# A transformer block with 32 routed experts on one core: token-wise gather, split scatter, reordered expert products and 4 MB weight loads

## The reference

```
h2 = rms_norm(x1, norm2_g, NORM_EPS).reshape(B * S, D)
logits = (x2 @ w_router + b_router)
top_vals, top_idx = lax.top_k(logits, TOP_K)          # 4 of 32 experts
top_w = jax.nn.softmax(top_vals, axis=-1)
combine = einsum('tk,tke->te', top_w, one_hot(top_idx, 32))
for e in range(32):
    h = x2 @ w_up[e] + b_up[e]                        # (256, 2048)
    glu, lin = h[..., :1024], h[..., 1024:]
    glu = minimum(glu, 7.0); lin = clip(lin, -7.0, 7.0)
    a = glu * sigmoid(1.702 * glu) * (lin + 1.0)
    out = out + combine[:, e:e+1] * (a @ w_down[e] + b_down[e])
return x1 + out
```

## Time and profile before

| what | value |
|---|---|
| time, median of 3 runs | 1219.95 us (1217.81 to 1220.06) |
| time of the profiled execution | 1219.87 us |
| span of the profiled execution | 1218.1 us |
| mean granted TensorE clock | 0.978 of full |
| PE busy | 1169.7 us (96%) |
| DVE busy, ACT busy | 339.1 us (28%), 266.9 us (22%) |
| HBM read | 448.12 MB, 369 GB/s over the span |
| front part, up to the first up product of item 1 | 288.8 us |
| item 1 to 32, up to the last down product | 288.8 to 1211.0 us |

### The profile page before, as it was taken

The page is one execution under the profiler, slowest core; times in us unless marked ns, Lnnn a source line. Parts: engine busy times, 40 slices in busy tenths (PEclk is TensorE's granted clock), DMA queues, the critical chain, the costliest instruction groups (busy, mean ns, idle before and its releaser), DMA issues.

```text
span 1218.1 us, 15891 instructions
## 1 busy us (share of the span) xinstructions
PE 1169.7 (96%) x6786; PEld 562.5 (46%) x6788; DVE 339.1 (28%) x625; ACT 266.9 (22%) x407; POOL 84.7 (7%) x101
## 2 busy tenths in 40 slices
PE   8999999997999999999999999999999999999998
PEld 7789988884333333333333333333333333333332
DVE  5767865655111111111111111111121111111112
ACT  6765454442111111111111111111111111111110
POOL 6333340001000000000000000000000000000000
PEclk9999999998999999999999999999999999999999
DMA  8454469858999999999999999999999999999991
GB/s 313 151 169 149 151 246 361 304 217 330 382 425 429 428 428 428 427 428 426 429 427 427 428 428 429 426 427 428 427 428 428 427 427 428 428 426 427 428 405 66
DMA packets 51476, 450.16 MB, mean 370 GB/s; under 512 B 4610, under 2 KB 4738, under 8 KB 26836
## 3 DMA queue, kind: packets, MB, share of 16 engines
q1 hardware_dynamic: 49936, 447.76, 89.1%
q10 hardware_dynamic: 1476, 1.42, 0.4%
HBM read 448.12 MB, written 1.05 MB: 369 GB/s over the span
## 4 chain that ended last, share of the span: by engine, by line
PE 85%; DVE 10%; ACT 2%; issue 1%; POOL 1%; DMA 0%; DVEq 0%; SPq 0%; POOLq 0%; ACTq 0%
PE aux L1604 37%; PE aux L1661 20%; PE acc L1448 11%; PE aux L1537 4%; PE acc L1441 3%; PE acc L1587 3%; PE aux L1635 2%; DVE lin L1228 2%; DVE sig L1232 2%; DVE glu L1224 2%; DVE lin L1225 2%; PE aux L1615 1%; DVE w_lo L880 1%; PE aux L1650 1%; PE aux L1644 1%
## 5 line engine op out<-in xcount | busy, mean ns | idle before, releaser
L1604 PE MATMUL aux<-ring,xgT 128*64 128x512 f32 x2048 | 458.2, 594 | 0.8 <-DVE xgT L1164 0.8
L1604 PEld LDWEIGHTS aux<-ring,xgT 128*64 128x64 f32 x2048 | 140.5, 137 | 266.4 <-issue 258.0
L1661 PE MATMUL aux<-ring,aT 128*64 128x512 f32 x1024 | 245.3, 635 | 0.0
L1224 DVE TENSOR_SCALAR glu<-aux 128x512 f32<-128x512 f32 x32 | 22.1, 692 | 483.3 <-PE aux L1604 483.3
L1661 PEld LDWEIGHTS aux<-ring,aT 128*64 128x64 f32 x1024 | 77.0, 147 | 148.7 <-issue 147.1
L845 ACT ACTIVATE sig<-glu 128x512 f32<-128x512 f32 x32 | 20.1, 630 | 474.9 <-DVE glu L1224 474.9
L880 DVE TENSOR_TENSOR w_lo<-raw,w_hi 128x1024 fp32r<-128x1024 f32 x80 | 104.3, 1324 | 50.0 <-ACT w_hi L662 50.0
L662 ACT ACTIVATE w_hi<-raw 128x1024 fp32r<-128x1024 f32 x80 | 84.1, 1059 | 88.6 <-PE acc L1448 73.0
L1587 PE MATMUL acc<-y_sb,pick_wT 64*128 64x512 f32 x256 | 98.2, 628 | 0.8 <-ACT y_sb L853 0.8
L1448 PE MATMUL acc<-w_hi,hT_hi 128*128 128x512 f32 x188 | 75.7, 403 | 1.4 <-DVE hT_lo L892 1.3
L1448 PE MATMUL acc<-w_hi,hT_lo 128*128 128x512 f32 x188 | 73.3, 390 | 0.0
(11 more groups left out here) (292 smaller groups left out, 920.1 us busy)
## 6 DMA issues: line engine op xcount, KB each, us to landing
ring<-w_up_dram SPq DMA_DIRECT2D x128, 2048.0 KB, 22.9
ring<-w_down_dram SPq DMA_DIRECT2D x64, 2048.0 KB, 21.9
raw<-w_in_dram SPq DMA_DIRECT2D x25, 1024.0 KB, 5.2
raw<-w_branch_dram SPq DMA_DIRECT2D x6, 1024.0 KB, 5.2
raw<-w_kv_dram SPq DMA_DIRECT2D x4, 1024.0 KB, 5.2
raw<-w_out_dram SPq DMA_DIRECT2D x4, 1024.0 KB, 5.3
x<-x_dram SPq DMA_DIRECT2D x2, 512.0 KB, 4.3
raw<-w_in_dram SPq DMA_DIRECT2D x2, 512.0 KB, 6.4
```

The source lines that it names most:

```text
L1224: nc.vector.tensor_scalar(glu[:], bank_glu[:], LIMIT, None, ALU.min).then_inc(glu_ready, 1)
L1604: ins = nc.tensor.matmul(bank[64 * half:64 * half + 64, :], xgT[:, k], w_rows[:, c0 + half * W:c0 + (half + 1) * W], start=(k == 0), stop= ...
L1661: ins = nc.tensor.matmul(bank_cy[64 * half:64 * half + 64, :], aT[:, j, 64 * ff_half:64 * ff_half + 64], w_rows[:, half * W:(half + 1) * W ...
```

## The change

- **Gather by tokens.** `x1` itself (float32) is the moving operand and `pick` (float32, scaled with the token's rstd) the stationary one: 4 products of 512 columns give the 64 gathered rows in `bank_cy`. ACT copies them to `xg_tok` (the room of `sig`), PE turns them with 4 transposes (`turn_gathered`), and DVE multiplies them into `xgT`. `m_parts` and the work that made it (ACT, POOL, DVE) go. The gather stands behind `k == 3`, the transposes behind `k == 5`.
- **Scatter.** The item's output is scaled by its weight per slot (`slot_w`) and split by ACT (`y_hi`) and DVE (`y_lo`) into two float32r parts; the scatter is 8 float32r products with a 0/1 matrix `pickT`, all behind the next item's up products. The two transposes of `pick_w` move into the middle of the down products.
- **Glu columns first.** For `k` 6 and 7 all products of `bank_glu` are issued before those of `bank_lin`, with a semaphore of their own (`glu_done`); DVE multiplies `glu` with the sigmoid before it clamps `lin`.
- **Match-replace.** The top-4 set is found with one `match_replace` per tile of tokens in place of index search, comparison and reduction.
- **Ring.** 12 units of 16 KB per partition; an expert is 2 chunks of `w_up` (4 MB, 32 KB per partition) and 2 of `w_down` (2 MB), 8 chunks (two experts) are held. The two first `w_up` chunks are loaded in halves.

```diff
-UP_ROWS, DOWN_ROWS = 2, 4
+UP_ROWS, DOWN_ROWS = 4, 4
 UP_CHUNKS, DOWN_CHUNKS = KD // UP_ROWS, KD // DOWN_ROWS
 CHUNKS = UP_CHUNKS + DOWN_CHUNKS
-RING = 11
-WARM_UP, KEEP_UP = 14, 8
-NEG = -1.0e30
+UNITS, CHUNK_UNITS = 12, (2, 2, 1, 1)
+RING = 2 * CHUNKS
+FIRST_UNIT = [UNITS // 2 * (s // CHUNKS) + sum(CHUNK_UNITS[:s % CHUNKS]) for s in range(RING)]
+HALVED = 2
...
                     src = w_down[bass.ds(expert, 1), c * n:(c + 1) * n, :].rearrange("o (p j) n -> p (o j n)", p=P)
-                sp.dma_start(ring[:, slot], src).then_inc(slot_loaded[slot], 16)
+                sp.dma_start(chunk_tile(slot), src).then_inc(slot_loaded[slot], 16)
 
             def load_next(g):
                 load_chunk(g % RING, g % CHUNKS, g // CHUNKS)
@@ -460,22 +468,20 @@
                     sp.wait_ge(aux_ready, JOB["mem_y", MEM_H - 1] + 1)
                     block_read(sp, ("cb",))
                 if p in (27, 29, 31, 33):
-                    load_next((p - 27) // 2)
+                    n = (p - 27) // 2
+                    load_half_chunk(n // 2, n % 2)
                 if p == 35:
                     sp.wait_ge(half_used, 2 * LAST_PIECE[("proj", 1, 1)] + 2)
...
+            sp.wait_ge(half_used, 2 * NP)
             load_next(5)
-            for g, last in ((6, NP - 3), (7, NP - 1)):
-                sp.wait_ge(lo_done, 2 * last + 2)
-                load_next(g)
-            sp.wait_ge(half_used, 2 * NP)
-            load_next(8)
-            load_next(9)
+            load_next(6)
             sp.wait_ge(logits_ready, 1)
-            sp.wait_ge(parts_pool, 2)
-            sp.wait_ge(parts_dve, 2)
-            load_next(10)
+            load_next(7)
             for g in range(RING, NEXP * CHUNKS):
                 chunk_used(sp, g - RING)
...
-                nc.scalar.activation(top_e[:, t], top_v[:, t, 0:TOPK], ACT.Exp, bias=ntop[:, t:t + 1],
-                                     accum_out=top_den[:, t, 0:1]).then_inc(soft_ready, 1)
-
-
-            nc.scalar.activation(aT[:, 0], ident[:], ACT.Copy).then_inc(aT_ready, 1)
-            nc.scalar.activation(y_sb[:, 0:P], ident[:], ACT.Copy).then_inc(y_ready, 1)
...
+
+            copy_gathered(1)
 
             def item(n):
+                copy_gathered(n + 1)
+                act.wait_ge(xg_turned, n + 1)
                 act.wait_ge(glu_ready, n)
                 nc.scalar.activation(sig[:], glu[:], ACT.Sigmoid, scale=ALPHA).then_inc(sig_ready, 1)
                 act.wait_ge(aT_done, n)
                 nc.scalar.activation(aT[:].rearrange("p k s -> p (k s)"), bank_t[:], ACT.Copy).then_inc(aT_ready, 1)
-                act.wait_ge(pick_wT_done, n)
-                act.wait_ge(scattered, 4 * n)
-                nc.scalar.activation(pick_wT[:].rearrange("p t s -> p (t s)"), bank_t[:, 0:NT * P],
-                                     ACT.Copy).then_inc(pick_wT_ready, 1)
+                act.wait_ge(pickT_ready, n)
                 act.wait_ge(y_done, n)
-                nc.scalar.activation(y_sb[:], bank_cy[:], ACT.Copy).then_inc(y_ready, 1)
+                nc.scalar.activation(y_hi[:], bank_cy[:], ACT.Copy, scale=slot_w[:, 0:1]).then_inc(y_hi_ready, 1)
 
...
-                ins = nc.vector.max_index(top_i[:, t], top_v[:, t], logits[:, t])
+                ins = nc.vector.match_replace(out=others[:, t], in_to_replace=top_v[:, t], in_values=logits[:, t],
+                                              imm_value=-HUGE)
             chained(ins)
-            chained(nc.vector.tensor_copy(top_f[:], top_i[:]))
+            nc.vector.tensor_scalar(chosen3[:, :, 0], others[:], -HUGE, None, ALU.is_equal).then_inc(chosen_ready, 1)
...
+            def move_gathered(n):
+                dve.wait_ge(xg_turned, n)
+                order = "p (h q) -> p q h"
...
+                dve.wait_ge(glu_done, n)
+                nc.vector.tensor_scalar(glu[:], bank_glu[:], LIMIT, None, ALU.min).then_inc(glu_ready, 1)
+                dve.wait_ge(glu_ready, n)
+                dve.wait_ge(sig_ready, n)
+                nc.vector.tensor_tensor(sig[:], glu[:], sig[:], ALU.mult).then_inc(gated_ready, 1)
                 dve.wait_ge(up_done, n)
-                nc.vector.tensor_scalar(glu[:], bank_glu[:], LIMIT, None, ALU.min).then_inc(glu_ready, 1)
-                nc.vector.tensor_scalar(lin[:], bank_lin[:], LIMIT, -LIMIT, ALU.min, ALU.max).then_inc(up_read, 1)
-                dve.wait_ge(glu_ready, n)
-                dve.wait_ge(up_read, n + 1)
-                nc.vector.scalar_tensor_tensor(lin[:], lin[:], 1.0, glu[:], ALU.add, ALU.mult
-                                               ).then_inc(glin_ready, 1)
-                dve.wait_ge(glin_ready, n)
-                dve.wait_ge(sig_ready, n)
-                nc.vector.tensor_tensor(sig[:], lin[:], sig[:], ALU.mult).then_inc(a_ready, 1)
-
-                dve.wait_ge(gathered, n + 1)
-                move_gathered()
+                nc.vector.tensor_scalar(bank_lin[:], bank_lin[:], LIMIT, -LIMIT, ALU.min, ALU.max
+                                        ).then_inc(lin_ready, 1)
+                dve.wait_ge(gated_ready, n)
+                dve.wait_ge(lin_ready, n)
+                nc.vector.scalar_tensor_tensor(sig[:], bank_lin[:], 1.0, sig[:], ALU.add, ALU.mult
+                                               ).then_inc(a_ready, 1)
+
+                move_gathered(n + 1)
+                build_pick_w(bass.ds(n - 1, 1))
                 build_pick(bass.ds(n + 1, 1))
+
                 dve.wait_ge(pick_wT_done, n)
-                build_pick_w(bass.ds(n, 1))
+                nc.vector.tensor_scalar(pickT[:].rearrange("p t s -> p (t s)"), bank_t[:, 0:NT * P], 0.0, None,
+                                        ALU.is_gt)
+                nc.vector.tensor_reduce(slot_w[:], bank_t[:, 0:NT * P], AX, ALU.add).then_inc(pickT_ready, 1)
                 dve.wait_ge(y_done, n)
                 build_bias_sel(bass.ds(n, 1))
+                dve.wait_ge(pickT_ready, n)
+                dve.wait_ge(y_hi_ready, n)
+                nc.vector.scalar_tensor_tensor(y_lo[:], bank_cy[:], slot_w[:, 0:1], plain_f32(y_hi[:]),
+                                               ALU.mult, ALU.subtract).then_inc(y_lo_ready, 1)
...
+            def gather(n):
+
+                pe.wait_ge(pick_ready, n)
...
-                                                   stop=(t == NT - 1 and m == 2), skip_group_check=True)
+                    for half in range(2):
+                        ins = nc.tensor.matmul(bank_cy[64 * half:64 * half + 64, :], pick[:, t],
+                                               x1[:, t, half * W:(half + 1) * W],
+                                               start=(t == 0), stop=(t == NT - 1), skip_group_check=True)
                 ins.then_inc(gathered, 1)
 
...
-            pe.wait_ge(extra_ready, 1)
-            nc.tensor.matmul(acc[3][:], zeros_bf[:, 0:P], zeros_bf[:], start=True, stop=True).then_inc(scattered, 1)
+            def turn_gathered(n):
+
+                pe.wait_ge(xg_tok_ready, n)
+                for q in range(KD // 2):
+                    c, j = q // UP_ROWS, q % UP_ROWS
+                    n = UP_ROWS * P
+                    rows = xg_tok[:, c * n:(c + 1) * n].rearrange("s (p j) -> s j p", j=UP_ROWS)[:, j]
+                    ins = nc.tensor.transpose(bank_cy[:, q * P:(q + 1) * P], rows, ident[:])
...
+            def scatter(n, opening=False):
+
+                pe.wait_ge(pickT_ready, n)
+                pe.wait_ge(y_hi_ready, n)
+                pe.wait_ge(y_lo_ready, n)
+                for t in range(NT):
+                    for part in (y_hi, y_lo):
+                        for half in range(2):
+                            s = slice(64 * half, 64 * half + 64)
+                            ins = nc.tensor.matmul(acc[2 * t + half][:], pickT[s, t], part[s, :],
+                                                   start=opening and part is y_hi, stop=True, skip_group_check=True)
+                            if part is y_lo:
+                                ins.then_inc(scattered, 1)
+
...
+                    if k == 3:
+                        if not first_item:
+                            pe.wait_ge(y_hi_ready, n - 1)
+                            pe.wait_ge(y_lo_ready, n - 1)
+                        gather(n + 1)
+                    if k == 5:
+                        turn_gathered(n + 1)
+
+                for bank, c0, done in ((bank_glu, 0, glu_done), (bank_lin, FF, up_done)):
+                    for k in range(KD - 2, KD):
+                        ins = up_product(k, bank, c0)
+                    ins.then_inc(done, 1)
 
                 if not first_item:
-                    scatter(n, range(3))
+                    scatter(n - 1, second_item)
                 pe.wait_ge(a_ready, n)
...
+                    if m == 3:
+                        pe.wait_ge(pick_w_ready, n)
+                        for t in range(NT):
+                            ins = nc.tensor.transpose(bank_t[:, t * P:(t + 1) * P],
```

(2 more changed lines are left out.)

322 lines of the change are left out of this document (134 added, 188 removed).

## The result

| | before | after | forecast |
|---|---|---|---|
| median of 4 runs each | 1218.88 us (1217.57 to 1220.06) | 1282.08 us (1281.21 to 1282.96) | 1252 (1216 to 1267) |
| ratio | 1 | 1.0519 [1.0501, 1.0537] | 1.026 |
| span, granted clock | 1218.1 us, 0.978 | 1279.3 us, 0.955 | |

A forecast was written before the change was run, and what follows sets the result against it. PE was taken to set the pace, with loads hidden. Before's span 1218.1 + 22.7 (items) - 4.4 (start) + 0.3 (end) + 13.4 (clock) = 1250.1 us, forecast 1252 us; range 1216 to 1267, clock falling in no item to all.

The forecast's parts named there:

- the clock term: Half-clock stretches at the down products: 8 items more, 21 of 30, at 1.68 us each, +13.4 us.
- the rival without slow items: PE dense enough that the clock never falls: 1213.2 us of span, 1215 us; chance 0.10.
- U to the transposes, +0.24 forecast: From the last up product's end (U) to the transposes of `sig`: 3.16 us against 2.92, the table load delaying the sigmoid.
- Transposes to down products, -0.81: From the transposes of `sig` to the down products only the copy to `aT` stays: 1.53 us against 2.34.
- Gather, turn, `pick_w` transposes, +1.28: PE time per item: gather plus 0.23 us, turning `xg_tok` 0.68, two `pick_w` transposes inside the down products 0.37.
- Item at full clock, 28.76: Sum of the steps in an item: +0.71 us on 28.05, 28.76 us per item, +22.7 us over 32 items.
- Start, -4.4: Item 1 starts about 4.4 us earlier, without the `x1s` and `m_parts` work and with a shorter selection.
- "all" as a rival: The clock falls in every item: 17 more than now, +28.6, 1265.3 us of span, 1267 us; chance 0.12.
- Loads: Loads stay hidden: last one lands at 1195 us, a floor of 1211 us, 39 us under the forecast.
- my rival had 1213 us: The table load doesn't delay the sigmoid: -41.6 us, held by the loads' floor at 1211, so 1213 us; chance 0.06.
- The drain: At each ACT table switch the skill's rule adds about 1380 ns; none was seen, with it 1296 us.

The follow-up runs named there:

- e2: Changed kernel with nine dummy bf16 products (fillers) behind the scatter, in PE's pause ahead of the transposes of `sig`: 1230.29 us.
- e11: Changed kernel with six fillers (dummy bf16 products) behind the scatter, in PE's pause ahead of the transposes: 1229.64 us.
- e1: Changed kernel with a one-column sigmoid at the top of ACT's item loop, so the table load runs early: 1202.42 us.
- e10: Kernel before with four fillers in the middle of the up products, where PE is busy: 1266.69 us.
- e8: Kernel before with one more DVE operation ahead of the sigmoid product, which makes PE's pause 1.40 us: 1245.71 us.
- the third question: Why all items are slow where 21 of 30 were forecast; runs e8, e9, e11, e12, e6, e10, e13 and e14 vary pauses, fillers and item length.
- e5: Changed kernel with `w_up` back in 2 MB chunks: 1281.52 us.
- e9: Changed kernel with four fillers behind the scatter, in PE's pause ahead of the transposes: 1283.11 us.
- e15: e1 (early table load) with `w_up` back in 2 MB chunks, no fillers: 1200.59 us.
- e13: e9 with one more filler behind the bias products, in the second pause, ahead of the down products: 1282.56 us.
- e14: e9 with one more filler in the middle of the up products: 1274.05 us.
- e12: e9 with two more fillers behind the bias products, in the second pause, ahead of the down products: 1235.20 us.
- e6: Changed kernel with nine fillers in the middle of the up products, where PE is busy, not in the pause: 1345.74 us.
- e3: e1 (early table load) with four fillers in PE's pause ahead of the transposes: 1202.17 us.
- e7: e3 with `w_up` back in 2 MB chunks: 1200.23 us.

## Why the prediction was wrong

The direction, the bound (PE, not the loads) and the mechanism in the item were right; the clock term was mis-sized, and the full-clock item came out a little short. Both were needed to leave the stated range, which took the clock from no slow item to all and gave the rest of the sum no width. With all items slow it ended at 1267 us, and the other 13 us are the item's length, item 1, the start and the slow place in item 32. For the same reason the rival without slow items was too low: e2 and e11, where no item from the second on is slow, took 1230 us where it had 1215.

- **U to the transposes, +0.24 forecast.** The table load waits for `glu_ready` and costs 1.30 us (826.62 to 827.92), as worked out; e1 confirms it by removal (1.28 us per item). Measured 3.35 us, forecast 3.16: ACT started 0.76 us behind DVE, not 0.73; the product with the sigmoid followed the sigmoid's start at 0.73 (827.92 to 828.65), not 0.67; and the last product followed the clamp of `lin` in PSUM at 0.80 (829.26 to 830.06), not 0.71, inside the bound of 0.1 per step that I had given and then left out of the sum.
- **Transposes to down products, -0.81.** 1.44 us (830.80 to 832.24) against the 1.53 of item 1: right.
- **Gather, turn, `pick_w` transposes, +1.28.** 1.71, 0.68 (853.91 to 854.59) and 0.37 us (837.50 to 837.87) from start to start: right. The transposes of `pick_w` cost more than their own 0.37, as the next point shows.
- **Item at full clock, 28.76.** e2 and e11 show 29.05, and over 32 items this is 9 us of the miss. The first two steps are 0.1 of it; 0.2 lie in the down products, which two transposes now cut in half. Timeline of PE of e11:

```profile
805.49 3.65 PE L1646 MATMUL aux<-ring,aT 128*64 128x512 f32 x16 [0.35 <-ACT aT L837]
809.08 0.44 PE L1657 MATMUL aux<-ident,pick_w 128*128 128x128 f32 x2
809.45 3.65 PE L1646 MATMUL aux<-ring,aT 128*64 128x512 f32 x16
812.93 1.89 PE L1576 MATMUL aux<-ring,xgT 128*64 128x512 f32 x8
```

  From 805.49 to 812.93 are 7.44 us, 7.07 without the transposes' 0.37; in one piece the same products took 6.87 before (1060.40 to the next item's first product at 1067.27).
- **Start, -4.4.** -3.3 measured: selection, gather and turn took 1.1 us longer, partly because a slow stretch from 279.3 us on fell on the gather (3.28 us for what takes 1.89 later). The terms that I named there, 3.1 + 1.5 - 0.3, make 4.3 and not 4.4.
- **Clock, +13.4: the step that failed.** I counted 13 slow items in 30 before, saw that the stretch with little work grew, and put 8 more on top, with "all" as a rival at 0.12. The 8 came from no row; only the sign did. "All" came true: 18 more in items 2 to 32, +30 us. That the stretch with little work is where the clock is lost was right (e2 and e11 fill it, and the 52 us are gone). What was wrong is to take the count before for a degree that grows with that stretch: e10 gets from 13 to 21 with the stretch unchanged, and e8, with a longer pause alone, has 20 and not 31. How item and slow stretches keep step enters as well. The item that I forecast, 28.76 + 1.68 = 30.44 us, was close to 30.7, and nothing that I had read in the trace of before gave 30.7 a meaning. The rival's span, 1265.3 us, with 9 for the item's length, 1.7 for the slow place in item 32 that it had not counted, 1.1 for the start and 1.5 for item 1 is 1278.6 of the 1279.3 us. Why all items are slow in this kernel is shown only as far as the third question goes.
- **Loads.** Hidden, as forecast (e5: the chunk size changes nothing). The floor was forecast at 1213 us and is 1202 (e1): in e1 the last loads land at 1182 us, where I had 1195. At 428 GB/s a chunk takes 4.90 us and not 4.94, which is 7.5 us for 188 of them; the other 5 us I have not traced. So with the load early the change gains 1.3%, where my rival had 1213 us.
- **The drain.** The Trainium skill, "ScalarE: Activation LUTs" (What ACT_TABLE_LOAD costs), gives 1283 ns for the load and a drain of some 1380 ns with it. The trace agrees on the load (1283 ns, 32 times, in the row of line 835 above) and again not on the drain: the activation follows the load's start at 1.30 us (826.62 to 827.92).

## What to carry to other kernels

A table load sits where the first activation of another set sits, behind that activation's wait; a one-column activation of the right function at the top of the loop moves it out of the way (80 us here), and the order of the instructions shows the fault before anything runs. In a loop with a pause on TensorE, count the slow places and look at their distance. Here, where it equalled the item, shortening the pause by about half gave nothing (e9) and the next 0.4 us everything (e11), so one filler count that fails does not show that fillers fail. Two changes that the eye takes for one, here the reordering and the bigger chunks, are to be timed apart: the first was worth -17 us once mended (e15), the second nothing, or 2 us of loss (e1 against e15, at the edge of what the runs can tell).

## What the runs showed of the hardware that was not expected

- The slow places can keep step with a loop for a whole run: 31 of 31 items of 30.72 us (after; e9 and e13 the same, with up to five fillers inside the pauses; e5 30.73 us).
- More work can be faster: one filler among the up products, which made the item 0.47 us longer, took 6 to 9 us off (e9 to e14), and a second one, for 0.12 us per item, behind the bias products 47 us (e13 to e12).
- A slow place of 3.4 us cost 1.6 to 1.7 us wherever it fell on products. In e6 some were 6.8 us long.
- With loads of 4 MB in packets of 32 KB for `w_up` the queue moved 428 to 431 GB/s mid-run (e1, e3), with loads of 2 MB 426 to 428 (e15, e7), and the run was not faster for it.
- Two transposes of 128x128 float32 in the middle of 32 records of down products cost 0.57 us of PE time (7.44 us in e11 against 6.87 before), 0.37 of it from start to start.
